# The 31-tap convolution of a mixer: from two engines to TensorE alone, with dense weights and shifted copies

## The reference

```python
    proj = jnp.einsum("bsd,dc->bsc", h, w_in)
    ...
    a = diff_attention(q, k, v, lam)
    a = rmsnorm(a, subln_g) * (1.0 - lam_init)
    ...
    c = u[..., :CV_WIDTH] * jax.nn.sigmoid(u[..., CV_WIDTH:])
    c = causal_dwconv(c, cv_dw_w) + cv_dw_b.astype(c.dtype)
    c = jax.nn.silu(layernorm(c, cv_ln_g, cv_ln_b))
```

## Time and profile before

| | us |
|---|---|
| Median of 3 runs | 1279.83 (1279.47 to 1279.92) |
| Profiled execution, its own time | 1277.17 |
| Its span in the trace | 1275.4 |
| PE, DVE, ACT, POOL busy in the span | 1239.7, 776.0, 590.5, 753.3 |

### The profile page before, as it was taken

The page is one execution under the profiler, slowest core; times in us unless marked ns, Lnnn a source line. Parts: engine busy times, 40 slices in busy tenths (PEclk is TensorE's granted clock), DMA queues, the critical chain, the costliest instruction groups (busy, mean ns, idle before and its releaser), DMA issues.

```text
span 1275.4 us, 16982 instructions
## 1 busy us (share of the span) xinstructions
PE 1239.7 (97%) x6162; PEld 1032.8 (81%) x6162; DVE 776.0 (61%) x1271; ACT 590.5 (46%) x964; POOL 753.3 (59%) x864
## 2 busy tenths in 40 slices
PE   5999999999999999999999999999999999999997
PEld 4777878878888888887778988887888888888887
DVE  5868788436554466798877436764367516641654
ACT  3375667457774446233456654444334323331341
POOL 2634444434344676686446977436559958875782
PEclk9999999999999999999999999999999999999998
DMA  9422224232345633232224443212313332333322
GB/s 379 180 67 76 85 83 140 97 100 87 121 132 191 215 111 99 83 101 86 85 69 163 138 146 116 83 50 82 93 58 108 116 108 84 98 100 99 99 83 67
DMA packets 43108, 142.73 MB, mean 112 GB/s; under 512 B 4881, under 2 KB 7441, under 8 KB 41873
## 3 DMA queue, kind: packets, MB, share of 16 engines
q1 hardware_dynamic: 42768, 141.39, 34.1%
q10 hardware_dynamic: 256, 0.26, 0.1%
HBM read 130.88 MB, written 8.39 MB: 109 GB/s over the span
## 4 chain that ended last, share of the span: by engine, by line
PE 70%; DVE 20%; ACT 6%; issue 3%; POOL 1%; DMA 1%; DVEq 0%; SPq 0%; ACTq 0%; POOLq 0%
PE ps L126 69%; DVE tm L139 5%; ACT tm L133 3%; DVE tm L136 3%; DVE ma L139 1%; DVE ac L139 1%; ACT L133 1%; PE ps L130 1%; DVE spl L136 1%; DVE sph L147 1%; DVE tm L144 1%; DVE x L139 1%; DVE ewl L136 1%; DVE zh L147 1%; DMA x<-xin 1%
## 5 line engine op out<-in xcount | busy, mean ns | idle before, releaser
L136 POOL TENSOR_TENSOR wl<-raw,wh 128x256 fp32r<-128x256 f32 x804 | 695.8, 897 | 463.8 <-ACT wh L133 456.2
L133 ACT ACTIVATE wh<-raw 128x1024 fp32r<-128x1024 f32 x201 | 212.1, 1056 | 307.2 <-PE ps L126 301.3
L126 PE MATMUL ps<-hh,wh 128*128 128x512 f32 x872 | 344.2, 395 | 0.0
L126 PE MATMUL ps<-hh,wl 128*128 128x512 f32 x872 | 340.4, 390 | 0.0
L126 PE MATMUL ps<-hl,wh 128*128 128x512 f32 x872 | 340.4, 390 | 0.0
L126 PEld LDWEIGHTS ps<-hh,wl 128*128 128x128 f32 x872 | 164.1, 188 | 34.8
L126 PEld LDWEIGHTS ps<-hh,wh 128*128 128x128 f32 x872 | 164.2, 188 | 33.3 <-DVE tm L139 0.4
L126 PEld LDWEIGHTS ps<-hl,wh 128*128 128x128 f32 x872 | 164.3, 188 | 33.0
L139 DVE SCALAR_TENSOR_TENSOR tm<-cb,par_sb,tm 128x512 f32<-128x512 f32 x88 | 87.1, 990 | 50.5 <-ACT tm L133 47.1
L136 DVE TENSOR_TENSOR tm<-tm,tm 128x512 f32<-128x512 f32 (+4 forms) x113 | 93.3, 830 | 40.1 <-ACT tm L133 37.3
L133 ACT ACTIVATE tm<-tm 128x512 f32<-128x512 f32 (+3 forms) x109 | 54.1, 531 | 80.4 <-DVE tm L139 64.3
(11 more groups left out here) (308 smaller groups left out, 2254.0 us busy)
## 6 DMA issues: line engine op xcount, KB each, us to landing
raw<-units SPq DMA_DIRECT2D x201, 512.0 KB, 3.5
ada<-units SPq DMA_DIRECT2D x16, 512.0 KB, 14.7
kept<-ge SPq DMA_DIRECT2D x16, 256.0 KB, 3.0
tm<-kept SPq DMA_DIRECT2D x16, 256.0 KB, 3.7
tm<-gate_w SPq DMA_DIRECT2D x12, 256.0 KB, 4.2
x<-xin SPq DMA_DIRECT2D x2, 1024.0 KB, 6.3
x<-xin SPq DMA_DIRECT2D x1, 2048.0 KB, 11.2
out<-x SPq DMA_DIRECT2D x16, 128.0 KB, 1.8
```

The source lines that it names most:

```text
L126: return self.none if self.e is None else self.e.matmul(out, lhs, rhs, start=start, stop=stop, skip_group_check=skip)
L133: return self.none if self.e is None else self.e.activation(out, in_, func, **kw)
L136: return self.none if self.e is None else self.e.tensor_tensor(out, a, b, op)
```

## The change

- PE does all four channel groups. A weight unit `("cw", j)` now serves a whole group j: four of them instead of eight. Channels are taken as 32 x 4 (channel 4c + g): for each g the rows of the weights hold 32 channels at four shifts (4a), the columns 32 channels at four shifts (m), and two matrices (o = 0 and 16) reach the 31 taps. So for each g and o there are 3 products on two halves of 258 columns: 48 matmuls of 258 columns for a group j, 192 in all. `conv(j, part)` does half of them, 24.
- The rows need shifted copies: `spread_rows(j)` on SP copies the 128-partition tiles `USh` and `USl` by eight transfers into `MVh` and `MVl`, each to 32 partitions x 4 x 532 numbers. ACT copies PSUM to `E` (`conv_out`, eight copies of 258 columns for each j), `gather_rows(j)` on SP brings the four shifts back to 128 partitions by four transfers of 256 KB, and DVE adds them up in three instructions (`join(j)`).
- `conv(j, part)` stands earlier: `conv(0, .)` and `conv(1, .)` around the projections `u` 6 and `u` 7, `conv(2, .)` and `conv(3, .)` between the four `dv` units and after them. Nothing is put between the parts of the attention in place of the 16 halves. `CW_HALVES` and `TAP_STEPS` go.
- The transfers stand in SP's order among the weight loads: `spread_rows(0)` ahead of the load nine units after `u` 4, and so on. With `spread_rows(1)` SP also waits for `s_xn` 7, the last of eight DVE instructions that scale `X`.

```diff
@@ order of the weight units
-    u += [("u", 4 * x + j) for j in range(4) for x in range(2)]
-    u += [("dv", i) for i in range(4)]
-    u += [("dq", 0), ("cw", 2, 0), ("dk", 0), ("cw", 2, 1), ("dq", 1)]
+    u += [("u", 0), ("u", 4), ("u", 1), ("u", 5), ("u", 2), ("cw", 0), ("u", 6), ("u", 3), ("cw", 1), ("u", 7)]
+    u += [("dv", 0), ("cw", 2), ("dv", 1), ("dv", 2), ("cw", 3), ("dv", 3)]
+    u += [("dq", 0), ("dk", 0), ("dq", 1)]
@@ PE
+        def conv(j, part):
+            s, p = PLACE["cw", j] % RING, j % 2
+            if part == 0:
+                pe.wait_ge(l_mv[p], j, 3, 1)
+                pe.wait_ge(s_wh, ("cw", j))
+            for g in (2 * part, 2 * part + 1):
+                banks = conv_banks(j, g)
+                for b in banks:
+                    take(b)
+                for o in (0, 1):
+                    w = slice(256 * g + 128 * o, 256 * g + 128 * o + 128)
+                    cols = [slice(258 * y + 16 * o, 258 * y + 16 * o + 258) for y in range(2)]
+                    for y, b in enumerate(banks):
+                        pe.mm(PS[b][:, 0:258], WH[s][:, w], MVh[p][:, g, cols[y]], o == 0, False)
...
+            if j >= 2:
+                conv(j - 2, 0)
             if j:
                 hproj("m", ("u", 4 + j), b1)
             bank[b1] = (s_ux, (j, 1))
-        vproj("d", "dv", "m")
+            if j >= 2:
+                conv(j - 2, 1)
+        def conv_beside(u):
+            if u:
+                conv(2 + u // 3, (u + 1) % 2 if u < 3 else 0)
+        vproj("d", "dv", "m", conv_beside)
+        conv(3, 1)
...
         dproj(0, 0)
         dproj(0, 1)
-        conv(0)
         dproj(0, 2)
-        conv(1)
         dproj(0, 3)
         dproj(0, 4)
-        conv(2)
         dproj(0, 5)
-        conv(3)
@@ ACT
+            for g in (2 * part, 2 * part + 1):
...
+                for y, b in enumerate(conv_banks(j, g)):
+                    act.fn(E[j % 2][:, g, 258 * y:258 * y + 258], PS[b][:, 0:258], ACT.Copy).then_inc(*s_e.up(j, g, y))
+            if part:
+                refill(("cw", j))
@@ DVE
+        def join(j):
+            dve.wait_ge(l_tt[j % 2], j, 3)
+            dve.stt(AC[j][:, :], TT[0][:, :], pcol("cv_dw_b_2", j), TT[1][:, :], ALU.add, ALU.add).then_inc(*s_pair.up(j, 0))
+            dve.tt(TT[2][:, :], TT[2][:, :], TT[3][:, :], ALU.add).then_inc(*s_pair.up(j, 1))
+            dve.wait_ge(s_pair, j, 1)
+            dve.tt(AC[j][:, :], AC[j][:, :], TT[2][:, :], ALU.add).then_inc(*s_ac.up(j))
...
+            dve.cp(USh[j % 2][:, 30:30 + T], t1).then_inc(*s_cph.up(j))
+            dve.wait_ge(s_cph, j)
+            split_low(USl[j % 2][:, 30:30 + T], t1, USh[j % 2][:, 30:30 + T], (j,), s_cpl)
...
-            taps((0, 6, 6, 14)[j])
+        for j in range(3):
+            join(j)
         v_low("d", V2h, V2l)
...
+        join(3)
         dproj(0, 1)
-        taps(3)
@@ SP
+        def spread_rows(j):
+            p = j % 2
+            sp.wait_ge(s_pad, 2)
+            sp.wait_ge(s_cpl, j)
+            if j == 1:
+                sp.wait_ge(s_xn, 7)
+            if j >= 2:
+                sp.wait_ge(s_unit, ("cw", j - 2))
+            for a in range(4):
+                for x, (mv, us) in enumerate(((MVh[p], USh[p]), (MVl[p], USl[p]))):
+                    sp.dma(f32(mv[GROUP * a:GROUP * a + GROUP, :, :]),
+                           f32(us[:, 4 * a:4 * a + CONV_IN])).then_inc(*l_mv[p].up(j, a, x))
+        def gather_rows(j):
+            p = j % 2
+            if j:
+                sp.wait_ge(s_ac, j - 1)
+            sp.wait_ge(s_e, j, 3, 1)
+            for m in range(4):
+                sp.dma(TT[m][:, :], E[p][GROUP * m:GROUP * m + GROUP, :, m:m + T]).then_inc(*l_tt[p].up(j, m))
...
+            for n, unit in enumerate((("u", 4), ("u", 5), ("u", 6), ("u", 7))):
+                if j == PLACE[unit] + 2 * RING + 1:
+                    if n >= 2:
+                        gather_rows(n - 2)
+                    spread_rows(n)
+            for n, unit in ((2, ("dv", 1)), (3, ("dv", 3))):
+                if j == PLACE[unit] + 2 * RING + 1:
+                    gather_rows(n)
```

More of the change, by code:

```diff
@@ L1 @@
+import itertools
 from contextlib import ExitStack
@@ L236 @@
 OFF = [0, 512, 896, 1152]
-TAPS = [tuple(range(8 * q, min(8 * q + 8, 31))) for q in range(4)]
+GROUP = 32
+CONV_IN = 532
+CONV_OUT = 516
 C1 = 6.28125
@@ L341, in build @@
     cp0 = off[0]
[L342 to L350, removed]
+    PADDED = T + 32
+    USh = [at(f"ush{i}", [P, PADDED], F32R) for i in range(2)]
+    USl = [at(f"usl{i}", [P, PADDED], F32R) for i in range(2)]
+    o_yc = [cp0 + 4 * PADDED * j for j in range(4)]
+    o_ac = [off[0] + 2048 * j for j in range(4)]
+    AC = [at(f"ac{j}", [P, T], F32) for j in range(4)]
+    off[0] += 256
     LM = at("lm", [P, 384], F32, cp0 + 6912)
@@ L934, in dproj @@
             bank[b] = (s_rx, (nm, h, 2))
[L936 to L954, removed]
         def qk_d(n):
@@ L1353, in cq_bank, with conv_banks @@
         return 6 if f == 2 else f % 2
-    def cw_done(n):
-        return CW_BEFORE + sum(CW_HALVES[:n])
+    def conv_banks(j, g):
+        other = (2, 3) if j < 2 else (0, 1)
+        return ((6, 7), other)[g % 2] if g < 2 else (other, (6, 7))[g % 2]
     def square_tile(f, x=0, m=1):
@@ L1640, in scalar_program, with conv_beside @@
             act.fn(u_tile(j, 1)[:, :], u_tile(j, 1)[:, :], ACT.Sigmoid).then_inc(*s_us.up(j))
[L1641 to L1653, removed]
+            if j >= 2:
+                conv_out(j - 2, 1)
+        def conv_beside(u):
+            if u:
+                conv_out(2 + u // 3, (u + 1) % 2 if u < 3 else 0)
+        vproj("d", "dv", V2h, conv_beside)
         def dproj(h, step):
@@ L2344, in scale_x @@
                 dve.wait_ge(s_root, "m2", "out")
[L2345 to L2361, removed]
+                dve.stt(X[:, f, :], X[:, f, :], pcol("final_g", f), RB2[:, :], ALU.mult, ALU.mult).then_inc(*s_xn.up(f))
+        def join(j):
[4 more added lines that the diff above has]
+            dve.tt(AC[j][:, :], AC[j][:, :], TT[2][:, :], ALU.add).then_inc(*s_ac.up(j))
         for j in range(4):
@@ L2483, in vector_program @@
         dproj(1, 2)
-        taps(2)
         join_d(0)
@@ L2507, in vector_program @@
                     sub_high(h)
-            taps(TAP_STEPS[n])
             if n == 9:
@@ L2765, in pool_program @@
         pool.wait_ge(s_unit, ("wo", 7))
-        pool.zero(CPF[:, :, 0:30]).then_inc(*s_pad.up(0))
-        pool.zero(f32(CPAh[:, :, 0:30])).then_inc(*s_pad.up(1))
-        pool.zero(f32(CPAl[:, :, 0:30])).then_inc(*s_pad.up(2))
+        for p in range(2):
+            for t in (USh[p], USl[p]):
+                pool.zero(f32(t[:, 0:30]))
+                last = pool.zero(f32(t[:, 30 + T:PADDED]))
+        last.then_inc(*s_pad.up(2))
         pool.zero(RS[:, :]).then_inc(*s_pad.up(3))
@@ L2949, in pack_units @@
             b = np.zeros((128, U), np.float32)
-            for i, x in enumerate(TAPS[u[2]]):
-                np.fill_diagonal(b[:, 128 * i:128 * i + 128], w["cv_dw_w_2"][0][x, 128 * u[1]:128 * u[1] + 128])
+            taps = w["cv_dw_w_2"][0][:, 128 * u[1]:128 * u[1] + 128]
+            c = np.arange(GROUP)
+            for g, o, a, m in itertools.product(range(4), range(2), range(4), range(4)):
+                x = 4 * a + m + 16 * o
+                if x < 31:
+                    b[GROUP * a + c, 256 * g + 128 * o + GROUP * m + c] = taps[x, g::4]
         elif k == "wo2":
```

90 lines of the change are left out of this document (38 added, 52 removed).

## The result

| | median us | ratio to before |
|---|---|---|
| Before, 4 runs beside these | 1279.65 (1279.11 to 1279.92) | |
| After, 4 runs | 1339.24 (1335.71 to 1341.36) | 1.0463 [1.0435, 1.0491] |

The change makes the kernel slower by 59.6 us. The profiled execution of after is its run of 1335.71, with a span of 1333.9, 58.5 more than before; the forecast added 23.8.

The account below looks back on a forecast made before the run. PE was taken as the bound, busy 1239.7 of 1275.4 us. Matmuls +23.3, spreads +5.3, hold +7.0, attention -13.5 and clock +1.7 make +23.8: 1301.0 profiled, 1303 as median, range 1286 to 1316.

Parts of the forecast that it names:

- the waits of the attention: From `dk` 0 to `kv` 0: new PE waits, 28.0 with crowding, making the stretch 91.2 for 104.68, so -13.5.
- the clock behind the waits: At `dk` 0: PE's long stillness lowers its clock and slows the matmuls behind it, +1.7, between nothing and 5.4.
- the spreads: Ahead of `conv(0, 0)` to `conv(3, 0)`: PE waits for late `spread_rows` transfers, 0.8, 1.6, 2.0 and 0.9, together +5.3.
- 192 matmuls of 258 columns: New convolution on PE: eight parts at 2.91 each, +23.3.
- hold at `dk` 0: PE idles 12.6 until t + 21.0 (t: end of `dv`), as DVE's `join(3)` awaits the gather; net +7.0.
- the bound of 9.5: Upper bound for the spreads' waits, if transfers run at half of the 418 GB/s that loads reach.
- narrow transfers: Rival at spreads and gathers: 32 partitions pass half of 128's rate; spread waits 9.5, gather 2 later; 1309 to 1314; chance 0.20.
- no hold: Rival at `dk` 0: gather lands early or DVE's read-out passes, so 12.6 becomes 1.5; 1291; chance 0.12.
- the bounds of the hold, 9.8 and 15.5: Range of PE's idle time ahead of `dk` 0; 9.8 if the gather lands like a lone 512 KB load.
- The prediction's own test: Wrong if the gather lands by t + 9 or `dk` 0 to `kv` 0 falls under 80; 91 expected.
- The rival that the filler was not needed: Attention: PE runs as densely without convolution halves, so time follows the matmuls, 20.0 less; 1260; chance 0.10.

Follow-up runs that it names:

- e4_before_bare: The kernel before, with all 16 convolution halves and all remaining taps moved ahead of `dq` 0, so the attention has no filler; 1319.93 us, ratio 1.0317.
- e2_fill: The changed kernel plus 168 unused matmuls of constants at the 14 places where convolution halves stood; 1331.9 us, ratio 1.0408.
- e3_join_late: The changed kernel with `join(3)` on DVE moved behind the read-out of `dq` 0 and head 0's key rotation; 1327.07 us, ratio 1.0364.
- e1: Small program of transfers alone, no kernel, varying row length, pitch, order and partitions; a spread took 18.65 to 19.75 us narrow, 7.85 to 128 partitions.
- m2: Small program of transfers alone, no kernel, varying partition placement and source; a spread took 19.37 us to 64 side by side, 8.04 to 32 four apart.
- e5_strided: The changed kernel with spreads writing and gathers reading 32 partitions four apart instead of side by side; 1311.95 us, ratio 1.0246.
- e6: The changed kernel with only PE's order in the attention changed, projection work moved ahead of waits and keys through bank 1; 1309.18 us, ratio 1.0231.

## Why the prediction was wrong

The direction was right, and the waits of the attention were right in place, cause and length. The step that failed is the clock behind the waits: the sum had 1.7 for it, and about 26 was measured. With the spreads, which were mis-sized, that makes 58.5 in the span where the sum gave 23.8. By its own steps:

| step | forecast | measured |
|---|---|---|
| 192 matmuls of 258 columns | +23.3, 2.91 a part | 2.9 a part at full clock (546.07 to 548.97) |
| late spreads | +5.3 | +15.1 (8.9, 0.9, 5.3) |
| hold at `dk` 0 | idle 12.6, `dk` 0 at t + 21.0 | 13.4 idle, t + 22.0 |
| waits from `dk` 0 to `kv` 0 | 28.0 | 27.4 (109.66 - 82.22) |
| clock | +1.7 | about +26 |

- **The matmuls** and **the waits of the attention**: right, the second nearly place by place (3.52, 4.58, 3.72, 3.60, 3.71 ahead of the `pv_d`s for 3.5, 4.8, 3.6, 3.9, 3.5). That these waits are the filler's doing, and no conflict, e4_before_bare and e2_fill show.
- **The hold**: right in place and cause; 1.0 more, since the gather landed later. e3_join_late shows that DVE's order is the cause. The rival "no hold" is out: the gather landed 19.3 behind the end of `dv`.
- **The spreads**: wrong in size. The rate was taken from the copy of `kv`, 192 GB/s, on all partitions, and the bound of 9.5 from half of the loads' best. Measured is 2.18 MB in 19.4, 112 GB/s. This is the rival "narrow transfers", right in kind and too small in price; e1 and m2 show that the partitions side by side are all of it, and e5_strided that the waits go with them. +9.8. The sum was also unclear in itself: it priced 209 GB/s as slower than the 192 of `kv`, and its 15.7, 8.3, 8.6 and 6.5 come out only with a fixed part of some 2 us for each group of transfers, which it doesn't name (the bare rates give 16.8, 6.4, 8.2 and 4.6). How the bounds of the hold, 9.8 and 15.5, were reached it doesn't show.
- **The clock** is the step that failed. The sum gave it 1.7, for the one long stillness at `dk` 0, and there it was right: `dk` 0 took 7.1 instead of 5.6. Everywhere else it put the clock at nothing: it priced the waits for spreads, and those of 3.5 to 4.8 ahead of each `pv_d`, at their own length, without a reason. The trace of before had in fact no PE wait of that length in this stage (the longest is 1.66), so nothing in it showed what one would do. In after, the work from `dk` 0 to `kv` 0 took 82.2 instead of 63.2, 19.0 more. Of the lengthening ahead of `dk` 0, 15.0 beyond the forecast, 9.8 are waits for spreads and 5.2 are matmuls behind them: `conv(0, 0)` took 5.3 and `conv(2, 0)` 4.7 for 2.9. Behind `kv` 0 the work that lay between 679.73 and 740 before, 60.27, took 62.10, 1.8 more, at 0.98. Together 26.0 for 1.7, +24.3. With 9.8 for the spreads, 1.0 for the hold and -0.6 for the attention's waits this makes 34.5 of the 34.7 that the forecast lacked.

The 5.2 is what is left of the 15.0, not a reading of its own; the two parts of the convolution are 4.2 of it.

The prediction's own test, that it is wrong if the stretch from `dk` 0 to `kv` 0 falls under 80, looked to one side only; it came to 109.66, longer than with the filler in it. The rival that the filler was not needed is out by the same number.

What stays open: how the cost of the clock divides between the single waits. What the runs show is that it goes with the waits (0.98 in e2_fill, where they are covered) and makes up the 19.0 in the matmuls; when exactly the clock falls and how long it stays down differs between waits of one length, as in the fourth `pv_d` and in e4_before_bare. The experiments take whole groups of waits away (27.3 for spreads of 15.1; 30.1 for 11.5 less of waits in the attention and 4.5 less at the hold, with 4.9 more at the spreads), and their gains overlap by the medians: e3, e5 and e6 sum to 69.6, where all three give 57.0. By the profiled executions, of which after's is its fastest, they sum to 57.3 and all three give 54.9. Why narrow transfers within SBUF are slower than half, and from HBM are not, was not tried further.

## What to carry to other kernels

Matmuls that stand between the links of a chain over other engines may cost nothing: before they are made fewer or moved, add up the waits that they cover, and then price each such wait at its length and the slower matmuls behind it; here 27.4 of waiting brought 19.0 more. Where work has been made cheaper, leave some of it (or the next projection) in those places, and look at the order on the engines that release PE. Lay out a transfer that touches a quarter of the partitions so that these are spread over all 128.

## What the runs showed of the hardware

- A spread within SBUF of 2.18 MB took 19.4 us to 32 or to 64 partitions side by side, 8.0 to 32 that are 4 apart, 7.85 to 128. Reading has the same pattern, weaker: a gather took 7.4 from 32 side by side, 4.5 from 4 apart or from 128.
- With PE waiting for 3.5 to 4.6 us once in some 16 us, its clock was at 0.50 behind each of these waits for 3 to 8 us of work, and the mean over the 110 us was 0.78. In one case it fell only some 1.3 us after PE had resumed (behind 716.99), and it was at 0.50 also behind waits of 2.10 and 0.78 (636 to 642). The Trainium skill ("TensorE: Matmul & The Clock Gate", "Part 1: The HAM clock gate (the "warmup" mystery)") describes the same two levels, the slow one as the default that activity lifts; the trace agrees (0.50 in 683.50 to 686.00, 1.00 from 688).
- A kernel with 39 us more of matmuls ran 7 us shorter (e2_fill).
